# First branch's scores and value products as three fp32r products, with the value products, the dilated weights and four product tiles placed elsewhere

## What is computed

```
q_lat = einsum('bshd,hdc->bshc', a_q, w_uk)              # 8 heads, latent width 128
kv_lat = rmsnorm(a_kv, g_kv)
logits = einsum('bqhc,bqkc->bqhk', ql, kv_sel) * ATTN_SCALE + bias    # scores, branch A
o_lat = einsum('bqhk,bqkc->bqhc', softmax(logits), kv_sel)
o_a = einsum('bshc,hce->bshe', o_lat, w_uv)              # value product, per head 128 -> 64
...
alpha = softmax(stack(lses), axis=0)                      # branch C: the groups by their denominators
merged = sigmoid(z_a) * (o_a @ w_branch_a) + sigmoid(z_b) * (o_b @ w_branch_b) + sigmoid(z_c) * (o_c @ w_branch_c)
```

## Time and profile before

| what | value |
|---|---|
| time, median of 3 runs (lowest to highest) | 1014.67 us (1013.93 to 1016.5) |
| the profiled execution's own time | 1013.3 us |
| its span, first to last instruction | 1011.2 us |
| PE busy | 988.8 us, 98% of the span |
| DVE, ACT, POOL busy | 480.9, 381.0, 101.0 us |
| granted TensorE clock, mean | 0.998 of full speed |
| chain that ended last, by engine | PE 93%, issue 3%, others 1% each or less |

### The profile page before, as it was taken

How to read it: one execution, slowest core, us unless ns; L and a number is a source line. 1 busy time by engine, 2 the same in 40 slices (tenths; PEclk the granted TensorE clock), 3 DMA queues, 4 the chain that set the end, 5 groups by cost and what they waited for, 6 DMA issues and landing times.

```text
span 1011.2 us, 12639 instructions
## 1 busy us (share of the span) xinstructions
PE 988.8 (98%) x4897; PEld 805.0 (80%) x4897; DVE 480.9 (48%) x822; ACT 381.0 (38%) x675; POOL 101.0 (10%) x138
## 2 busy tenths in 40 slices
PE   6999999999999999999999999999999999999997
PEld 5778988878877777778788888988888888788885
DVE  3654778833235335663737374743443343231323
ACT  5354432255565566642222233442322322221222
POOL 1510000000045422200000002000000000000401
PEclk9999999999999999999999999999999999999999
DMA  8975225312130211165565652123344434222312
GB/s 324 267 235 161 84 84 153 117 43 84 63 107 22 65 30 32 33 208 171 172 198 166 218 210 84 63 84 104 104 115 157 143 104 145 84 104 84 125 42 83
DMA packets 88162, 123.11 MB, mean 122 GB/s; under 512 B 4824, under 2 KB 69941, under 8 KB 87986
## 3 DMA queue, kind: packets, MB, share of 16 engines
q1 hardware_dynamic: 87442, 115.98, 35.2%
q0 software_dynamic: 528, 6.22, 2.0%
q10 hardware_dynamic: 144, 0.26, 0.1%
HBM read 119.77 MB, written 8.45 MB: 127 GB/s over the span
## 4 chain that ended last, share of the span: by engine, by line
PE 93%; issue 3%; POOL 1%; ACT 1%; DVE 1%; DMA 1%; SPq 0%; POOLq 0%; ACTq 0%; DVEq 0%
PE tile_ps L830 19%; PE tile_ps L832 18%; PE tile_ps L831 18%; PE t_ps L1056 2%; PE s_ps L1038 2%; PE o_ps L1085 2%; PE o_ps L1234 1%; PE tile_ps L1234 1%; PE o_ps L1233 1%; PE s_ps L1234 1%; PE t_ps L1234 1%; PE tile_ps L1233 1%; PE s_ps L1233 1%; PE t_ps L1233 1%; PE o_ps L1232 1%
## 5 line engine op out<-in xcount | busy, mean ns | idle before, releaser
L830 PE MATMUL tile_ps<-h_hi,w_hi 128*128 128x512 f32 x736 | 292.6, 398 | 0.4
L832 PE MATMUL tile_ps<-h_hi,w_lo 128*128 128x512 f32 x736 | 287.2, 390 | 0.0
L831 PE MATMUL tile_ps<-h_lo,w_hi 128*128 128x512 f32 x736 | 286.8, 390 | 0.0
L1709 DVE TENSOR_TENSOR w_lo<-w_raw,w_hi 128x2048 fp32r<-128x2048 f32 (+3 forms) x61 | 133.0, 2181 | 161.5 <-ACT w_hi L1341 161.3
L830 PEld LDWEIGHTS tile_ps<-h_hi,w_hi 128*128 128x128 f32 x736 | 138.2, 188 | 37.3 <-issue 8.6
L832 PEld LDWEIGHTS tile_ps<-h_hi,w_lo 128*128 128x128 f32 x736 | 138.1, 188 | 29.4
L831 PEld LDWEIGHTS tile_ps<-h_lo,w_hi 128*128 128x128 f32 x736 | 138.3, 188 | 26.8 <-issue 0.2
L1341 ACT ACTIVATE w_hi<-w_raw 128x2048 fp32r<-128x2048 f32 (+3 forms) x62 | 111.1, 1792 | 45.2 <-PE tile_ps L832 9.1
L1706 DVE TENSOR_TENSOR t_lo<-t_raw,t_hi 128x2048 fp32r<-128x2048 f32 (+1 forms) x15 | 32.8, 2184 | 85.8 <-ACT t_hi L1339 85.8
L1479 ACT ACTIVATE nl<-nl,cst 128x256 f32<-128x256 f32 (+3 forms) x81 | 43.2, 534 | 49.9 <-DVE cst L1906 49.8
L1339 ACT ACTIVATE t_hi<-t_raw 128x2048 fp32r<-128x2048 f32 (+1 forms) x15 | 27.0, 1801 | 81.7 <-PE s_ps L1234 53.5
(11 more groups left out here) (372 smaller groups left out, 1684.5 us busy)
## 6 DMA issues: line engine op xcount, KB each, us to landing
w_raw<-in_w_in_dram SPq DMA_DIRECT2D x31, 1024.0 KB, 5.5
w_raw<-in_w_gate_up_dram SPq DMA_DIRECT2D x22, 1024.0 KB, 7.1
ada<-in_w_ada_dram SPq DMA_DIRECT2D x12, 1024.0 KB, 5.4
t_raw<-in_w_down_dram SPq DMA_DIRECT2D x10, 1024.0 KB, 5.0
row_copies<-row_flat POOLq DMA_DIRECT2D x1, 5632.0 KB, 20.9
ada<-in_w_ada_dram SPq DMA_DIRECT2D x8, 640.0 KB, 12.3
ada<-in_w_ada_dram SPq DMA_DIRECT2D x8, 512.0 KB, 4.4
ada<-in_w_ada_dram SPq DMA_DIRECT2D x8, 384.0 KB, 9.5
```

Of the source, the lines that this page charges most:

```text
L830: pe.matmul(dst[0:mw, :], wh, x_hi[:, kx, :], start=start, stop=False)
L831: pe.matmul(dst[0:mw, :], wh, x_lo[:, kx, :], start=False, stop=False)
L832: mm = pe.matmul(dst[0:mw, :], wl, x_hi[:, kx, :], start=False, stop=stop)
L1709: dve.tensor_tensor(w_lo[s][:, 0:kt, 0:n_cols], w_raw[s][:, 0:kt, 0:n_cols], w_hi[s][:, 0:kt, 0:n_cols].bitcast(F32), ALU.subtract) \
```

## The change

- Branch A's scores become three fp32r products. ScalarE writes `qlat` as fp32r (`latent_hi`), VectorE makes `q_lo` and frees the bank; `kv_T` and `kv_lo` are made once, and ScalarE moves `kv_lo` in step 36.
- `up_values` becomes three fp32r products. ScalarE writes `olat_hi`, VectorE makes `olat_lo`; `uv_hi` and `uv_lo` are made in steps 36 and 37. UV0 to UV4 move to other steps (UV0 40 to 41, UV1 46 to 45, UV2 48 to 49, UV3 stays in 54, UV4 56 to 57) and all of them stand ahead of the step's T and P. Their split follows in the same step.
- The two `oc` tiles are made in steps 49 and 57, not both in 49. Branch C's weights are made in steps 43 and 44, and merged in steps 45 to 48.
- ScalarE's two halves of w_hi for chunks 19 and 20 move half a step to a step earlier, behind the copy of the transposed block.
- The four tiles TL_Z, TL_Z+1, TL_Z+4 and TL_Z+5 go to the banks `s_ps0`, `s_ps1`, `t_ps0`, `t_ps1`, which are idle there; the tiles of each pair are made in the order 1, 0.

```
-STEP_OC = 49
+OC_STEPS = (49, 57)
...
 
-    return {36: 0, 42: 1, 44: 2, 50: 3, 52: 4, 56: 5, 60: 6, 64: 7}.get(p)
+    return {37: 0, 41: 1, 45: 2, 50: 3, 53: 4, 56: 5, 60: 6, 64: 7}.get(p)
 
 
...
-        kv_T = place("kv_T", R + 8, [P, S])
+        kv_T = place("kv_T", R + 8, [P, S], F32R)
+        kv_lo = [place(f"kv_lo{b}", R + at, [P, S], F32R) for b, at in enumerate((31, 49))]
+        olat_hi = place("olat_hi", R + 31, [P, S], F32R)
+        olat_lo = place("olat_lo", R + 65, [P, S], F32R)
-        qlat = [place(f"qlat{b}", R + 117.25 + 2 * b, [P, S]) for b in range(2)]
-        qlat.append(aq_T[:, 0, :])
+        qlat = [place(f"qlat{b}", R + at, [P, S], F32R) for b, at in enumerate((117.25, 119.25, 0))]
+        q_lo = [place(f"q_lo{b}", R + at, [P, S], F32R) for b, at in enumerate((97, 99, 57, 59, 61, 63))]
+        q_lo += q_lo[2:4]
+        uv_hi = place("uv_hi", R + 67, [P, A_H, DH], F32R)
+        uv_lo = place("uv_lo", R + 121.25, [P, A_H, DH], F32R)
...
+        def product_bank(t):
...
+            n = t - TL_Z
+            return {0: s_ps[0], 1: s_ps[1], 4: t_ps[0], 5: t_ps[1]}.get(n, tile_ps[t % 2])
...
-                if t >= 2:
+                if t in (TL_Z + 6, TL_Z + 7):
+                    wait_tile_out(pe, t - 4)
+                elif t >= 2:
                     pe.wait_ge(tile_out[b], k)
...
                     if i == 0:
                         wait_tile_out(pe, ATT_TILE["qlat", h])
-                    mm = pe.matmul(ps[:, 0:w], qlat[h % 3][:, i * P:(i + 1) * P], kv_T[:, 0:w], start=True, stop=True)
+                    if v == 40:
+                        pe.wait_ge(kv_moved, 1)
+                    q_h, q_l = (q[:, i * P:(i + 1) * P] for q in (qlat[h % 3], q_lo[h]))
+                    pe.matmul(ps[:, 0:w], q_h, kv_T[:, 0:w], start=True, stop=False)
+                    pe.matmul(ps[:, 0:w], q_l, kv_T[:, 0:w], start=False, stop=False)
+                    mm = pe.matmul(ps[:, 0:w], q_h, kv_lo[v >= 40][:, 0:w], start=False, stop=True)
                 else:
                     h, m = (v - MIX_B) // 4, k % 2
...
             def up_values(h):
                 b = tile_start(ATT_TILE["uv", h])
                 pe.wait_ge(olat_in, h + 1)
-                pe.matmul(tile_ps[b][0:DH, :], w_uv[:, h, :], olat[:], start=True, stop=True) \
+                if h == 0:
+                    pe.wait_ge(uv_split, 1)
+                pe.matmul(tile_ps[b][0:DH, :], uv_hi[:, h, :], olat_hi[:], start=True, stop=False)
+                pe.matmul(tile_ps[b][0:DH, :], uv_hi[:, h, :], olat_lo[:], start=False, stop=False)
+                pe.matmul(tile_ps[b][0:DH, :], uv_lo[:, h, :], olat_hi[:], start=False, stop=True) \
                     .then_inc(tile_made[b], 1)
 
...
+                for p in products_at(v):
+                    if uv_after(p) is not None:
+                        up_values(uv_after(p))
...
                 for p in products_at(v):
                     times_values(p)
-                    if uv_after(p) is not None:
-                        up_values(uv_after(p))
                 if len(qlat_at(v)) == 2:
                     for h in qlat_at(v):
                         latent_queries(h)
-                if v == STEP_OC:
-                    transpose_c(0)
-                    transpose_c(1)
+                if v in OC_STEPS:
+                    transpose_c(OC_STEPS.index(v))
                 if ob_at(v) is not None:
                     transpose_b(ob_at(v))
 
 
             four, of_c = straight[0:4], [(4, 0), (5, 1)]
-            project_two(chunk_z(0) + 3, TL_Z + 0, x=(oa_hi, oa_lo), kts=four)
+            s = chunk_ready(chunk_z(0) + 3)
+            for m in (1, 0):
+                project(s, TL_Z + m, oa_hi, oa_lo, four, m * P, bank=product_bank(TL_Z + m))
             wait_tile_out(pe, ATT_TILE["ob", 2])
             wait_tile_out(pe, ATT_TILE["ob", 3])
-            project_two(chunk_z(0) + 4, TL_Z + 2, x=(ob_hi, ob_lo), kts=four)
-            project_two(chunk_z(0) + 4, TL_Z + 4, x=(oc_hi, oc_lo), kts=of_c)
+            s = chunk_ready(chunk_z(0) + 4)
...
+                project(s, TL_Z + 4 + m, oc_hi, oc_lo, of_c, m * P, bank=product_bank(TL_Z + 4 + m))
             for g in range(1, 4):
                 ch, tl = chunk_z(g), tile_z(g)
                 project_two(ch + 0, tl + 0)
...
+            def latent_hi(h):
...
+                t = ATT_TILE["qlat", h]
+                wait_tile_made(act, t)
+                act.activation(qlat[h % 3][:], tile_ps[t % 2][:], ACT.Copy).then_inc(qlat_hi_made, 1)
...
-                for p in products_at(v - 1):
-                    if uv_after(p) is not None:
-                        h = uv_after(p)
-                        d0 = DH * (h % 2)
-                        split_hi(("uv", h), oa_hi[d0:d0 + DH, h // 2, :], DH)
...
-                    make_hi(n + 1, before[n] if n in before else ATT_TILE[dense_at(v - 2)[0]],
-                            kt=4 if n + 1 == chunk_z(0) + 3 or n in (18, 19) else KT, part=n in (18, 19))
-                if v >= 2 and chunk_starting_at(v - 2) in (18, 19):
-                    n = chunk_starting_at(v - 2) + 1
-                    act.activation(w_hi[n % 2][:, 4:KT, :], w_raw[n % 2][:, 4:KT, :], ACT.Copy) \
-                        .then_inc(w_hi_made[n % 2], 1)
+                    if n not in (18, 19):
+                        make_hi(n + 1, before[n] if n in before else ATT_TILE[dense_at(v - 2)[0]],
+                                kt=4 if n + 1 == chunk_z(0) + 3 else KT)
                 if len(qlat_at(v)) == 1:
-                    evacuate(ATT_TILE["qlat", qlat_at(v)[0]], qlat[qlat_at(v)[0] % 3][:, :])
+                    latent_hi(qlat_at(v)[0])
...
                     copy_transposed(t)
                 for p in products_at(v):
+                    if uv_after(p) is not None:
+                        h = uv_after(p)
+                        d0 = DH * (h % 2)
+                        split_hi(("uv", h), oa_hi[d0:d0 + DH, h // 2, :], DH)
+                if chunk_starting_at(v) in (18, 19):
+                    n = chunk_starting_at(v) + 1
+                    make_hi(n, ATT_TILE["bqk", 7] if n == 19 else ATT_TILE["bv", 3], kt=4, part=True)
+                if v and chunk_starting_at(v - 1) in (18, 19):
+                    n = chunk_starting_at(v - 1) + 1
+                    act.activation(w_hi[n % 2][:, 4:KT, :], w_raw[n % 2][:, 4:KT, :], ACT.Copy) \
+                        .then_inc(w_hi_made[n % 2], 1)
+                for p in products_at(v):
                     if MIX_A <= p < MIX_B and p % 4 == 3:
                         g = p // 4
                         act.wait_ge(o_made[g % 2], g // 2 + 1)
...
+                        act.activation(olat_hi[:], o_ps[g % 2][:], ACT.Copy).then_inc(olat_hi_made, 1)
...
                 if len(qlat_at(v)) == 2:
                     for h in qlat_at(v):
-                        evacuate(ATT_TILE["qlat", h], qlat[h % 3][:, :])
-                if v == STEP_OC:
-                    split_hi(("oc", 0), oc_hi[:, 0, :])
-                    split_hi(("oc", 1), oc_hi[:, 1, :])
+                        latent_hi(h)
+                if v == 36:
+                    act.wait_ge(wu_in, 32)
+                    act.activation(uv_hi[:], w_uv[:], ACT.Copy).then_inc(uv_hi_made, 1)
+                    act.activation(kv_lo[1][:], kv_lo[0][:].bitcast(F32), ACT.Copy).then_inc(kv_moved, 1)
+                if v in OC_STEPS:
+                    t = OC_STEPS.index(v)
+                    split_hi(("oc", t), oc_hi[:, t, :])
                 if ob_at(v) is not None:
...
 
             dve.wait_ge(kvt_made, 1)
-            dve.tensor_copy(kv_T[:], o_ps[1][:]).then_inc(kv_ready, 1)
...
+                    if uv_after(p) is not None:
+                        h = uv_after(p)
+                        d0 = DH * (h % 2)
+                        split_lo(n_split, ("uv", h), oa_lo[d0:d0 + DH, h // 2, :], oa_hi[d0:d0 + DH, h // 2, :], DH)
+                        n_split += 1
...
+
+                    if MIX_A <= p < MIX_B and p % 4 == 3:
+                        g, h = p // 4, (p - MIX_A) // 4
+                        dve.wait_ge(olat_hi_made, h + 1)
+                        dve.tensor_tensor(olat_lo[:], o_ps[g % 2][:], olat_hi[:].bitcast(F32), ALU.subtract) \
+                            .then_inc(olat_in, 1)
+                for h in qlat_at(v):
+                    t = ATT_TILE["qlat", h]
+                    dve.wait_ge(qlat_hi_made, h + 1)
+                    dve.tensor_tensor(q_lo[h][:], tile_ps[t % 2][:], qlat[h % 3][:].bitcast(F32), ALU.subtract) \
+                        .then_inc(tile_out[t % 2], 1)
+                if v == 37:
+                    dve.wait_ge(uv_hi_made, 1)
+                    dve.tensor_tensor(uv_lo[:], w_uv[:], uv_hi[:].bitcast(F32), ALU.subtract).then_inc(uv_split, 1)
...
                     link(dve.tensor_tensor(c_den, c_wgt[:, 0:16], c_wgt[:, 16:32], ALU.add))
+                if v == 44:
                     link(dve.reciprocal(c_den, c_den))
```

(3 more changed lines are left out.)

47 lines of the change are left out of this document (26 added, 21 removed).

## The result

The change makes the kernel slower, if by little: median 1016.78 us over 20 runs (1012.65 to 1018.2) against 1013.48 over 20, ratio 1.0024, 95% interval [1.0013, 1.0036]; a second job, both kernels executed again later, gave 1.0016 [1.0006, 1.0025]. One of the 20 executions of the kernel before took 1237.28 us and is left out of the ratio. The median lies outside the forecast range (1011.5 us, 1007.5 to 1015); the ratio lies inside the 0.3% that the forecast called no change, and its interval lies above 1, up to 0.36%. The profiled execution took 1012.65 us, span 1010.5, at a granted clock of 0.999, and is the fastest of the 20.

A forecast was written before the change was run, and what follows sets the result against it. The chain lies almost whole on TensorE, so its work and pauses count in full. Matmuls -5.9, pauses that go -4.2, end -1.2, pauses that come +8.7 give -2.6; 0.6 more off for recovery: 1011.5 us, range 1007.5 to 1015.

The forecast's parts named there:

- the 8.7 us for pauses that come: TensorE waiting on VectorE's new `olat_lo`, merge and `q_lo` work and UV4's split: 8.7 us, bounds 4 to 12.
- the 0.6 us taken off for recovery: Within a head, TensorE makes good part of its pauses: 0.6 us off the forecast time.
- the forecast -3.2: Whole kernel: terms sum to -2.6 us, another 0.6 off for recovery; median 1014.67 becomes 1011.5 us.
- Matmuls, -5.9: TensorE's fp32r products: scores 1.8, value products 1.4, narrow output 2.7, together 5.9 us saved (3.2 to 7.3).
- R3: Rival: the narrow 64-row output of value products still costs 0.34 with fp32r; 1.7 us lost, 1013.2 us; chance 0.12.
- The 128-column product: TensorE, branch A's scores: an fp32r product of 128 columns costs 0.12 us, not 0.06.
- R6: Rival: an fp32r product of 128 columns costs 0.06 us, scores gain 3.2 instead of 1.8; 1010.1 us; chance 0.06.
- The end, -1.2: End of attention: waits of the first `oa` product (1.0) and next z chunk (0.2) go, 1.2 us saved.
- Pauses that go, -4.2: TensorE's waits at UV2 and UV4, `oc` tiles, P(33), P(41), P(49) and `bv` behind `qlat` pairs go: 4.2 us.
- read long before: UV2 and UV4 in new steps find their tile's bank already read, so their waits go: 1.0 us.
- P(37), P(53) and P(57) lose nothing: Products behind `olat_lo`: a UV ahead covers the wait, TensorE arriving at 2.9 us against 2.7; no loss.
- R5: Rival: VectorE sets each head's time, 0.9 us in seven heads, 6.3 above forecast, 1017.8 us; chance 0.09.

The follow-up runs named there:

- all products plain: The change's new steps and four banks, with branch A's scores and value products plain fp32 as in the kernel before: 1010.61 us, ratio 0.9965 to the kernel before.
- `olat_lo` later: The changed kernel with `olat_lo` behind the next step's shift on VectorE, last head unchanged: 1009.85 us, ratio 0.9956 to the kernel before.
- plain value products: The changed kernel with branch A's value products alone plain fp32 again, scores still fp32r: 1011.51 us, ratio 0.9976 to the kernel before.

## Why the prediction was wrong

In short: the work saved on TensorE came as forecast (-6.1 for -5.9). The term that failed is the 8.7 us for pauses that come. About 12 us came, because the query pair of step 45 (2.3 us), UV4 (1.2) and UV5 (0.6) stood in no term, and the 0.6 us taken off for recovery did not come. At equal clock that makes +0.8 to +1.6 us out of the forecast -3.2. What is left up to 1016.78 goes with the lower clock of the first job, for which there was no term either.

Ends of records, added up by operation over nearly the same stretch of both profiles (TensorE, from the projections behind the selection of keys at 207 to the z projection at 465), show work and pauses apart:

| operation | before us | after us |
|---|---|---|
| scores, branch A | 19.5 | 15.9 |
| value products | 9.2, of which 1.2 pauses | 7.7, of which 2.2 pauses |
| query tiles | 5.3 | 8.1 |
| projections of bv and z, first products | 44.0 | 47.6 |
| whole stretch | 258.1 | 258.9 |

- **Matmuls, -5.9: right.** Scores -3.6, value products -2.5, together -6.1. The table counts what a plain score pays behind a UV (0.20) with the scores, six times, 1.2 us in all; the forecast had it with the value products. Both kernels pay some 0.2 for the score behind a query tile. The narrow output pays nothing with fp32r, by rows 0.00 for 0.34, so R3 is out. The rule of the Trainium skill that float32r matmuls force the full column group ("PSUM — Partial Sum Buffer", The four PSUM rules) fits that; no run here shows that it is the reason.
- **The 128-column product: right for a reason that doesn't hold.** It costs 0.11 (297.50 to 297.61), near the 0.12 that I took, and the three cost 0.29 by their ends, not 0.36. So R6 is out, and with it, for fp32r at this width, the 56 ns that the Trainium skill gives ("TensorE: Matmul & The Clock Gate", Wait — 56ns, not 53.3ns?). But my ground, that plain passes "stop falling at 0.11", misreads the rows: 0.43, 0.215 and 0.11 at 512, 256 and 128 columns fall in proportion. Plain passes show no such floor down to 128 columns; the fp32r product does, 0.12 at 256 and 0.11 at 128.
- **The end, -1.2: right**, -0.9 measured alone, and -1.3 in the profile.
- **The scores' part** (-1.8 in the forecast, `q_lo`'s waits +3.05, so +1.25): +0.7 to +0.8 measured. Right in size.
- **Pauses that go, -4.2: right; what the new steps bring in return: missing.** This is the first step that failed. With all products plain the waits at P(33), P(41), P(49), UV2, UV4 and behind the `oc` tiles are gone. But the same profile has four new ones: the sixth query tile waits 0.41 at 316.05 and parts its pair, 1.54 us in all, two `bv` parts come 0.57 and 0.50 late for `oa_lo` (328.28, 349.70), and a z part 0.43 (383.08). So the new steps gave -2.0 net, and not -4.2; their new pauses are among the 12 us of the next point. UV1 now stands ahead of the query pair of step 45 and shares a bank with its second tile. The forecast saw that UV1's split would hold somebody, and put it on the `bv` part behind (1.1 in step 46). It came at the tile itself.
- **Pauses that come, 8.7: the second and larger step that failed; mechanism right, list too short.** The profile of the change has about 12 us of them, the upper bound that I gave. Listed and found: P(45) 0.98 late (forecast 1.0), P(49) 0.99 (1.1), P(41) 0.34 (0.6), `bv` in steps 38, 50, 54 and 58 0.93, 1.63, 0.95 and 0.63 (1.2, 1.7, 0.75, 0.85), and 0.37 at UV6 where I had 0.4 at P(61). Not in the list: 2.3 at the sixth query tile (1.49 late and a lost overlap of 0.86, below), 0.5 at the query pair at 289.36, 1.19 at UV4, 0.64 at UV5, and 0.4 more than before at the z part at 382.41. UV4 waits at 345.96 for the `bv` part's evacuation, which queues on ScalarE behind an exponential (344.88) that waited for a shift (344.55) behind `olat_lo` (343.94, after 1.46 idle): so for UV4 "read long before" holds with plain products and fails with split ones. "P(37), P(53) and P(57) lose nothing" held. With 12 for 8.7 the sum is +0.5, and the profiles have +0.8 between the two matmuls.
- **The value products' part** by my terms (-4.1 of matmuls; 1.1, 1.0, 1.7, 0.6, 0.85 and 0.4 of waits) comes to +1.55; measured +3.7, or +3.1 in the profiles. It hangs on the place of one VectorE instruction: with `olat_lo` later the same part is worth -0.5 (-2.7 against -2.2 with plain value products).
- **0.6 off for recovery: none is seen.** The pauses add up in full.
- The sum: 2.2 us short in the new steps, 2.2 in the value products, 0.6 in recovery and 0.3 at the end, less 0.45 in the scores, make the 4.8 us between -3.2 and +1.6. R5 named the right engine, VectorE, but its price, 6.3, was not reached; heads keep their time where the forecast said so: S(40) to S(44) 306.13 - 297.35 = 8.8 (forecast 8.8), S(48) to S(52) 330.94 - 318.85 = 12.1 (11.9). The head between, S(44) to S(48), went from 11.7 to 12.7; it has the parted query pair.
- The first job's median lies another 2.1 us above the second's, at a mean clock of 0.9954 against 0.9975, which is 1.5 us at 0.72 us per 0.001. This the forecast had no term for, and why the clock was lower is open. Of the 0.8 us between +0.8 in the profiles and +1.6 in the fit, no run shows where it lies; it is about the fit's error.
